# First sample's prologue: key pages turned behind the differences, value taps added on GpSimd, prompt outputs moved apart from the sample's buffers

## The reference

```python
def _past_rows(cache, page_table, slot):
    rows = cache[page_table, :, slot]
...
def _compress(k, pe, w1, b1, w2, b2):
    B, L, KV, Dh = k.shape
    r = CMP_LEN // CMP_STRIDE            # 32 // 16 = 2
    nseg = -(-L // CMP_STRIDE)
...
    blk = jnp.concatenate([seg[:, j:j + n_cmp] for j in range(r)], axis=2)
    blk = blk + pe[:, None, :]
    flat = jnp.swapaxes(blk, 2, 3).reshape(B, n_cmp, KV, CMP_LEN * Dh)
    return jax.nn.gelu(flat @ w1 + b1) @ w2 + b2
```

## Time and profile before

| what | value |
|---|---|
| runs | 1097.58 us median of 3 (1095.91 to 1097.97) |
| profiled execution | 1091.5 us, its span from first to last instruction 1089.7 us |
| TensorE busy | 992.8 us, 91% of the span |
| VectorE, ScalarE, GpSimd busy | 592.9, 486.6, 83.2 us |
| mean granted clock of TensorE | 0.940 of full speed (2.4 GHz) |
| sample stage, first product on TensorE | 259.55 us |
| key scores of the first sample | 302.67 us |

### The profile page before, as it was taken

The page is one execution under the profiler, slowest core; times in us unless marked ns, Lnnn a source line. Parts: engine busy times, 40 slices in busy tenths (PEclk is TensorE's granted clock), DMA queues, the critical chain, the costliest instruction groups (busy, mean ns, idle before and its releaser), DMA issues. The chain is left out here.

```text
span 1089.7 us, 25951 instructions
## 1 busy us (share of the span) xinstructions
PE 992.8 (91%) x9553; PEld 871.0 (80%) x9553; DVE 592.9 (54%) x1304; ACT 486.6 (45%) x982; POOL 83.2 (8%) x59
## 2 busy tenths in 40 slices
PE   6799996776699999999999999799997999999997
PEld 3478894555578778787878787689997999999997
DVE  1600005541677777686868677686467755544324
ACT  3322224544246565565656473644442544443223
POOL 1134430000001010101000000000000000000000
PEclk9789997866899999999999999889998999999999
DMA  9788766713947777777777776566642444444401
GB/s 328 230 285 294 240 216 202 276 50 125 346 137 229 271 265 259 255 257 272 234 271 238 266 249 210 162 161 201 223 163 78 151 152 143 141 140 143 172 0 49
DMA packets 132533, 220.17 MB, mean 202 GB/s; under 512 B 20948, under 2 KB 76753, under 8 KB 127682
## 3 DMA queue, kind: packets, MB, share of 16 engines
q1 hardware_dynamic: 127586, 185.79, 51.6%
q0 software_dynamic: 4896, 33.68, 8.4%
HBM read 210.99 MB, written 12.58 MB: 205 GB/s over the span
## 5 line engine op out<-in xcount | busy, mean ns | idle before, releaser
L1258 PE MATMUL ps<-t_XT,t_slab 128*128 128x128 f32 x1024 | 148.2, 284 | 15.1 <-DVE t_XT L1710 14.8
L103 PE MATMUL ps<-b_uH,b_slabH 128*128 128x320 f32 x480 | 151.3, 315 | 8.8 <-DVE b_uL L2415 5.3
L1258 PEld LDWEIGHTS ps<-t_XT,t_slab 128*128 128x128 f32 x1024 | 130.3, 196 | 32.9 <-issue 24.0
L104 PE MATMUL ps<-b_uL,b_slabH 128*128 128x320 f32 x480 | 150.5, 314 | 0.0
L105 PE MATMUL ps<-b_uH,b_slabL 128*128 128x320 f32 x480 | 149.7, 312 | 0.0
L2303 DVE TENSOR_TENSOR b_slabL<-t_slab,b_slabH 128x2048 fp32r<-128x2048 f32 (+1 forms) x52 | 109.3, 2124 | 63.9 <-ACT b_slabH L2196 63.8
L2196 ACT ACTIVATE b_slabH<-t_slab 128x2048 fp32r<-128x2048 f32 (+1 forms) x52 | 92.3, 1784 | 94.4 <-PE ps L105 88.4
L103 PEld LDWEIGHTS ps<-b_uH,b_slabH 128*128 128x128 f32 x480 | 92.2, 192 | 10.3 <-issue 6.6
L104 PEld LDWEIGHTS ps<-b_uL,b_slabH 128*128 128x128 f32 x480 | 92.4, 192 | 0.0
L105 PEld LDWEIGHTS ps<-b_uH,b_slabL 128*128 128x128 f32 x480 | 92.0, 192 | 0.0
L1729 DVE STREAM_TRANSPOSE t_Kr<-t_Kr 128x512 f32<-128x512 f32 x128 | 80.1, 676 | 9.7 <-DMA t_Kr<-cache_moba_kv 8.6
(11 more groups left out here) (396 smaller groups left out, 2011.4 us busy)
## 6 DMA issues: line engine op xcount, KB each, us to landing
t_Kr<-cache_moba_kv SPq DMA_DIRECT2D x132, 256.0 KB, 3.0
t_Vr<-cache_moba_kv SPq DMA_DIRECT2D x124, 256.0 KB
t_slab<-w_ada SPq DMA_DIRECT2D x22, 1024.0 KB, 7.7
t_slab<-w_gu SPq DMA_DIRECT2D x22, 1024.0 KB, 5.2
t_slab<-w_in SPq DMA_DIRECT2D x17, 1024.0 KB, 5.7
t_slab<-w_down SPq DMA_DIRECT2D x11, 1024.0 KB, 5.0
t_slab<-cmp_w SPq DMA_DIRECT2D x2, 2048.0 KB
t_wkv<-cache_nsa_win SPq DMA_DIRECT2D x8, 512.0 KB, 4.5
```

What stands on the lines that cost most here:

```text
L103: pe.matmul(out, w_high, x_high, start=start, stop=False, **kw)
L104: pe.matmul(out, w_high, x_low, start=False, stop=False, **kw)
L1258: return pe.matmul(out[:, P * j:P * j + P], taps(w, j, lp)[:, P * ht:P * ht + P], XT[:, w, lp, j, :, :].rearrange("p v i -> p (v i)"), sta ...
```

## The change

Line numbers of the changed program are 3 or 4 higher at the same places.

- VectorE's prologue has a new order: the keys' taps are added in two halves, quarter 0's and quarter 1's differences stand ahead of all key pages, five pages stand ahead of the first selected scores, three between the differences of quarters 2 and 3, and eight behind these.
- The values' taps are added by GpSimd in a single instruction, the first that it runs in the block; TensorE waits for it (`taps_added`) after the first key scores.
- In memory `t_oT_p` is moved to the end of the prompt block's tensors, behind a gap of 3400 floats a partition, and `t_Vr`, the value pages, to the end of the sample block's. So only `t_Vr` has addresses in common with `t_oT_p`. VectorE and ScalarE no longer wait for the stores; SyncE waits for them behind the window's load, ahead of the first value pages.

```diff
+GAP = 3400
...
             load_queries(0)
             for q in range(4):
                 load_k(0, q)
+            load_window(0)
             sp.wait_ge(t["o_spilled"], 64)
-            load_window(0)
             for q in range(3):
                 load_v(0, q)
...
+            pool.tensor_tensor(added[:, 1, :, :], w1[:, 1, 0:8, :], w1[:, 1, 8:16, :], ALU.add).then_inc(taps_added, 1)
             for b in range(NB):
                 for q in range(4):
                     after = (b, q + 2) if q < 2 else (b + 1, q - 2)
...
             key_scores(None, 0)
+            pe.wait_ge(taps_added, 1)
             pe.wait_ge(om_taken, 1)
...
             act.wait_ge(zeroed, 4)
-            act.wait_ge(t["o_spilled"], 64)
             stage_queries(0)
...
-            dve.wait_ge(t["o_spilled"], 64)
             dve.memset(qa[:, :], 0.0).then_inc(zeroed, 1)
...
-            for q in range(4):
-                add_taps(0, slice(2 * q, 2 * q + 2))
-                if q == 3:
-                    add_taps(1, slice(6, 8))
+            add_taps(0, slice(0, 4))
+            for q in range(2):
                 segment_differences(None, q, 0)
                 segment_differences(None, q, 1)
-                if q < 3:
-                    add_taps(1, slice(2 * q, 2 * q + 2))
-                if q == 1:
-                    take_selected(0, 0)
-                turn_keys(0, range(4 * q, 4 * q + 4))
+            add_taps(0, slice(4, 8))
+            turn_keys(0, range(0, 5))
+            take_selected(0, 0)
+            for q in range(2, 4):
+                segment_differences(None, q, 0)
+                segment_differences(None, q, 1)
+                turn_keys(0, range(5, 8) if q == 2 else range(8, 16))
             take_selected(0, 1)
...
-                                    ("Sc_p", [P, 256]), ("PTc_p", [PSEG, 2 * H, P]), ("oT_p", [P, 4, 4, SEQ]),
+                                    ("Sc_p", [P, 256]), ("PTc_p", [PSEG, 2 * H, P]),
                                     ("nmax_p", [P, 3, H]), ("sum_p", [P, 3, H]), ("rsum_p", [P, H]),
-                                    ("cstat_p", [P, 2 * H])]:
+                                    ("cstat_p", [P, 2 * H]), ("gap_p", [P, GAP]), ("oT_p", [P, 4, 4, SEQ])]:
...
-            for name, shape in [("Kr", [P, 16, 512]), ("Vr", [P, 4 * KEPT_SLOTS, 512]),
+            for name, shape in [("Kr", [P, 16, 512]),
...
-                                ("join", [P, 64]), ("Om", [P, P]), ("On", [64, 2, DH]), ("Os", [P, DH])]:
+                                ("join", [P, 64]), ("Om", [P, P]), ("On", [64, 2, DH]), ("Os", [P, DH]),
+                                ("Vr", [P, 4 * KEPT_SLOTS, 512])]:
```

More of the change, by code:

```diff
@@ L1046, in decode_block @@
     win_landed, zeroed = sem("d_win"), sem("d_zeroed")
-    q_landed, keys_turned = sem("d_q"), sem("d_keys_turned")
+    q_landed, keys_turned, taps_added = sem("d_q"), sem("d_keys_turned"), sem("d_taps_added")
     filled, scored, small_mm, hidden_mm, keys_mm, out_mm, v_used = (
```

## The result

The changed kernel takes 1084.19 us in the median of four runs (1081.32 to 1090.65) against 1097.43 before: a ratio of 0.9898, 95% interval 0.9874 to 0.9922, so 8.6 to 13.8 us faster. Forecast were 1086.5 us and a gain of 11.1. The profiled execution took 1083.33 us, with a span of 1081.5.

What follows compares the result with a forecast made beforehand. The sample stage's prologue was taken to be bound by key pages once VectorE's order changed. Key scores 11.1 us sooner, other terms 0, took the profiled 1091.5 to 1080.4; adding the runs' 6.1 gave 1086.5 us, range 1083 to 1092.

Steps and rivals of the forecast that it cites:

- both terms of 0: Prologue: VectorE's and ScalarE's start 2.0 us sooner, and GpSimd's 4.61 us add, were each put at 0 us of effect.
- The cover named for the 2.0 us: Stage's start: VectorE's wait for key pages hides the 2.0 us earlier start; without that cover it would gain 2.0.
- The bound taken for it: Key page 8's landing time after issue: between 3.0 and 6.9 us; 6.7 taken, so it lands at 277.0.
- VectorE's chain: VectorE's queue from page 8's landing to the last turned page: 277.0 to 291.0, 14.0 us instead of 24.6.
- TensorE's tail: TensorE's work from quarter 2's differences to the key scores: 8.76 us, so scores start at 291.5.
- the signs of being wrong that the prediction named: Long add with late gather; VectorE standing for pages beyond 278 or after 286; last two quarters over 8 us; first pass over 52.0.
- The third gather's effect: Third gather, issued about 279, slows the last key pages to 6.9 us from 4.4; gain 10.8 instead of 11.1.
- Everything gained arrives at the end: Behind the prologue nothing has slack, key scores follow 52.0 us apart, so its whole gain of 11.1 us reaches the end.
- Half clock: Rival: TensorE runs the last two quarters at 1.2 GHz, costing 3.6 us; gain 7.5, time 1090.1; chance 0.12.
- Late pages: Rival: page 8 lands 3 to 8 us late, gathers sharing DMA engines; gain 3 to 8, 1090 to 1094; chance 0.04.
- No change: Rival: prologue ends early but the first pass waits for value pages until the 11 us are gone; 1097.6; chance 0.03.
- slower: Rival: page 8 lands after 288, delaying scores and differences behind five pages, or passes lengthen; up to 1104; chance 0.04.

Runs made afterwards that it cites:

- the old waits: Changed kernel with the three waits for the prompt's stores put back where they were, memory as changed; ratio to the kernel before 0.9889.
- pages last: Changed kernel with VectorE's first selected scores and differences of quarters 2 and 3 ahead of all 16 key pages; ratio to the kernel before 0.9924.
- the combined kernel: Changed kernel, values' taps on VectorE, quarter 2's and 3's differences each ahead of eight pages, second sample's gathers held, four value pages late; ratio to before 0.9899.
- the taps on VectorE: Changed kernel with the values' taps added by VectorE ahead of the key pages, without TensorE's wait for them; ratio to the kernel before 0.9878.

## Why the prediction was right, and where it was not

*The mechanism* was the named one. The order gives the gain, with the old waits as without them and with the taps on either engine; the waits and GpSimd's add give none, as both terms of 0 had it. The cover named for the 2.0 us, the key pages, is what hides them.

*The prologue* was forecast at 291.5 − 259.55 = 31.95 us and took 34.49. Page 8 was put 277.0 − 262.44 = 14.6 us behind the first issue and came 16.6 behind it: 2.1 of the 2.5 us. This is the mis-sized term. The bound taken for it, 6.9 us, was the longest landing in one profile, where the gathers left 5.1 and 9.2 us behind the first page. With both moved 2 and 3 us up the page took 8.5 and 8.3 us in the two profiles; but it took 7.9 with the gathers unmoved in the second profile of before, so the bound was short even without the move. VectorE's chain was right within 0.4 us, and TensorE's tail took 292.74 − 283.45 = 9.3 for 8.76, with part of quarter 2 at half clock: the granted clock was 0.50 from 282 to 288. Of the signs of being wrong that the prediction named, two came: counted from the stage's start VectorE stood for pages up to 277.78 + 1.30 = 279.1, beyond 278, and the first pass was longer than 52.0. The third, the last two quarters over 8 us, came at its border (284.70 to 292.74, 8.04).

*The third gather's effect*, worked out as 0.3 us less gain by the rule of the Trainium skill (DMA: Bandwidth & Descriptors, section on queues, rings and completion order), had its size right and its place wrong. The last page took 7.0 us, where the rule's sum has 6.9 and the forecast 4.4. But the pages did not bind in the changed kernel: VectorE had no stand at its second eight. With pages last they did bind, landing 26.3 us behind.

*Everything gained arrives at the end* was the step that failed in the first profile: "scores to scores is a fixed pass" isn't so for the first pass. The late instruction load costs 1.02 us of key scores there, and 3.3 in the combined kernel, and half clock behind a stand costs 2.4 with pages last. In the second profile of the changed kernel the pass is 52.00.

*The time* came nearer than the parts deserve. The profile of before was 6 us below the median of its runs, the changed kernel's 0.9 below its own. So the profiled time was missed by 2.9 us (1080.4 forecast, 1083.33), the median by 2.3 on the other side. Distances within the stage give 7.7 and 10.7 us for the two pairs of profiles; where the rest of the medians' 13.2 lies is not settled, as the stage's start alone moved by 6.4 us between executions.

*The rivals.* Half clock: in part, most of the 0.5 us by which TensorE's tail was longer, where the rival had 3.6. Late pages: the main part of the prologue's shortfall, 2.1 us and so below the rival's 3 to 8. No change and slower: neither. That pages standing first can cost time shows in the run with the waits gone and the old order.

## What to carry to other kernels

In an engine's in-order queue, work that waits for a transfer belongs behind all work that another engine waits for; here that was worth some 9 us, and a start 2 us earlier nothing. Before counting an earlier start as harmless, list which transfers it moves beside the one that binds. A shortened prologue can pay again behind its end: look there at the granted clock first, as a stand just before may be followed by work at 1.2 GHz (6.03 us of stand, 2.4 us lost in the key scores), and then for "issue" stands and the instruction queue's packets.

## What the runs showed of the hardware

- VectorE's add of two tensors in SBUF does not run beside GpSimd's add of two: it took 4.62 us in the changed kernel and ended 1.08 us behind the end of GpSimd's (259.35 + 4.62 against 258.24 + 4.65), 2.57 with the old waits (it ended at 263.55, 1.09 behind GpSimd's 262.46), and 1.19 alone. The Trainium skill (SBUF — State Buffer, section "Who interferes with whom") says that a VectorE instruction with two SBUF inputs contends with a GpSimd instruction that reads SBUF, over ports that are locked for one of the two; both runs agree. It cost nothing here: TensorE's first compression products start 8.02 us behind the stage's start in the changed kernel (266.27) and with the taps on VectorE (265.81) alike.
- A 256 KB page load took 8.5 us beside two gathers, where in the earlier trace rows it took 3.0 with none.
- What I take for TensorE's instruction load, one packet of 0.02 MB on queue q8, came up to 4.5 us into the key scores. At a granted clock of 1.00 the 128 key products took 4.47 us with it at their start and up to 7.76 with it late. In six executions TensorE's last four weight loads stood until 1.3 to 1.5 us behind the packet's end; that the packet causes the longer scores is read from this, no run delayed it alone. The Trainium skill (Runtime: NRT & Kernel Launch, section "Instruction fetch mechanics") says that an engine's sequencer refills its instruction memory in blocks of 16 KiB through a DMA queue of its own, and that this is mostly hidden; the packet's size agrees, while here up to 3.3 us were not hidden. What makes the sequencer ask for it, when, and what holds it back, no run shows.
- Behind stands of 6.03, 5.69 and 4.42 us TensorE began the key scores at a granted clock of 0.50 (1.2 GHz). The whole 128 products took 6.87 us in the first of these, against 4.47 at 1.00.
